# The S5 input products of a hybrid decoder trunk: plain float32, two parts per visit, in place of split products part by part

## The reference

```python
bu = jnp.einsum('blgh,gph->blgp', ug.astype(jnp.complex64), b_bar)
state = linear_scan(jnp.broadcast_to(lam_bar, bu.shape), bu)
y = jnp.einsum('blgp,ghp->blgh', state, c_c).real + d.astype(f32) * ug
```

## Time and profile before

| | |
|---|---|
| median of 3 runs | 2974.36 us (2973.3 to 2975.58) |
| profiled execution | 2973.05 us |
| its span, first to last instruction | 2971.0 us |
| mean granted TensorE clock | 0.993 |
| TensorE busy | 2894.8 us, 97% |
| VectorE busy | 2010.5 us, 68% |
| ScalarE busy | 1582.0 us, 53% |
| GpSimd busy | 751.4 us, 25% |
| DMA | 522.69 MB, mean 176 GB/s |

### The profile page before, as it was taken

The page is one execution under the profiler, slowest core; times in us unless marked ns, Lnnn a source line. Parts: engine busy times, 40 slices in busy tenths (PEclk is TensorE's granted clock), DMA queues, the critical chain, the costliest instruction groups (busy, mean ns, idle before and its releaser), DMA issues.

```text
span 2971.0 us, 56245 instructions
## 1 busy us (share of the span) xinstructions
PE 2894.8 (97%) x16280; PEld 2454.7 (83%) x16280; DVE 2010.5 (68%) x3316; ACT 1582.0 (53%) x2828; POOL 751.4 (25%) x813
## 2 busy tenths in 40 slices
PE   6999999999999999999989999999999999999997
PEld 5878888888888888888877788888888888888886
DVE  7788888755555667555568888887555555665555
ACT  5555554565555655444455554546555655644443
POOL 3145445401000123111123544543000011221110
PEclk9999999999999999999999999999999999999998
DMA  6655555655555556777745555555555555577775
GB/s 225 213 174 159 162 159 154 170 170 168 159 158 164 165 156 195 209 214 209 206 142 174 167 162 159 159 162 171 171 157 164 160 168 154 158 213 209 215 209 176
DMA packets 276414, 522.69 MB, mean 176 GB/s; under 512 B 30912, under 2 KB 33872, under 8 KB 275280
## 3 DMA queue, kind: packets, MB, share of 16 engines
q1 hardware_dynamic: 257360, 477.13, 54.8%
q10 hardware_dynamic: 18944, 44.18, 4.5%
HBM read 508.60 MB, written 16.78 MB: 177 GB/s over the span
## 4 chain that ended last, share of the span: by engine, by line
PE 46%; DVE 2%; issue 2%; ACT 1%; DVEq 0%; POOL 0%; ACTq 0%; POOLq 0%
PE ps L294 26%; PE ps L293 13%; PE ps L443 1%; PE ps L337 1%; DVE w L975 1%; PE ps L456 0%; PE ps L452 0%; PE ps L296 0%; PE ps L325 0%; PE ps L338 0%; DVE zb L1523 0%; PE ps L326 0%; PE ps L327 0%; PE ps L304 0%; PE ps L313 0%
## 5 line engine op out<-in xcount | busy, mean ns | idle before, releaser
L294 PE MATMUL ps<-hb,w 128*128 128x512 f32 x5824 | 2059.1, 396 | 7.3 <-POOL hb L1553 6.1
L975 DVE TENSOR_TENSOR w<-raw,w 128x512 fp32r<-128x512 f32 x1760 | 1290.2, 738 | 859.5 <-ACT w L590 845.1
L590 ACT ACTIVATE w<-raw 128x512 fp32r<-128x512 f32 x1760 | 1098.2, 629 | 1138.6 <-PE ps L294 1135.9
L293 PE MATMUL ps<-hb,w 128*128 128x256 f32 x5690 | 1632.4, 287 | 13.2 <-DVE w L975 11.8
L294 PEld LDWEIGHTS ps<-hb,w 128*128 128x128 f32 x5824 | 1092.9, 188 | 250.5 <-issue 6.7
L293 PEld LDWEIGHTS ps<-hb,w 128*128 128x128 f32 x5690 | 1076.0, 189 | 70.8 <-issue 29.3
L294 PE MATMUL ps<-gl,w 128*128 128x512 f32 x640 | 226.6, 395 | 0.0
L1576 POOL TENSOR_TENSOR xx<-g,tab 128x512 f32<-128x512 f32 x64 | 121.0, 1891 | 269.6 <-DVE g L1038 269.1
L1703 POOL TENSOR_TENSOR nf<-zb 128x256 f32 (+1 forms) x60 | 51.9, 864 | 537.1 <-DVE zb L1491 531.6
L294 PE MATMUL ps<-w,hb 128*128 128x512 f32 x512 | 180.8, 395 | 0.0
L293 PE MATMUL ps<-gl,w 128*128 128x256 f32 x560 | 156.6, 280 | 0.0
(11 more groups left out here) (296 smaller groups left out, 2582.1 us busy)
## 6 DMA issues: line engine op xcount, KB each, us to landing
raw<-in_w SPq DMA_DIRECT2D x1763, 256.0 KB, 2.8
mlaw<-in_mlaw ACTq DMA_DIRECT2D x16, 768.0 KB, 4.2
mlaw<-in_mlaw ACTq DMA_DIRECT2D x16, 512.0 KB, 3.5
gate<-xres ACTq DMA_DIRECT2D x32, 256.0 KB, 4.5
xres<-zb ACTq DMA_DIRECT2D x32, 256.0 KB, 3.7
zb<-in_x SPq DMA_DIRECT2D x8, 512.0 KB, 7.5
xres<-in_x SPq DMA_DIRECT2D x4, 1024.0 KB, 7.0
s5w<-in_s5w ACTq DMA_DIRECT2D x16, 256.0 KB, 3.5
```

The source lines that it names most:

```text
L293: mm(acc[:, T:], a_lo, m_hi, start=False, stop=False, skip_group_check=True)
L294: last = mm(acc, a_hi, m_both, start=(k == 0), stop=(k == nk - 1), skip_group_check=True)
L590: A(w2[:, d, :, 0, :], raw[:, s, :, :], ACT.Copy).then_inc(hi_ready, 1)
L975: V.tensor_tensor(w2[:, d, :, 1, :], raw[:, s, :, :], w2[:, d, :, 0, :].bitcast(F), ALU.subtract).then_inc(w2_ready, 1)
```

## The change

The three products on float32r halves are replaced by one plain float32 product, straight from `s5w` and from a float32 copy `us` of the inputs, still on 32 rows. A visit makes two parts: an even one into bank 4, and the odd one behind it into bank 7. There are two visits per iteration, after chunk 13 (parts 2 and 3) and after chunk 29 (parts 0 and 1 of the next iteration). `s5_split`, `bhi`, `blo` and the semaphore `us_split` are gone, and so is ScalarE's copy of the matrices; its copy of the inputs stays. `s5_next` moves from chunk 12 to chunk 17, and waits for the second visit, since the visits now read `s5w` themselves. `bu_ready` counts two per iteration in place of four.

```diff
-        us = sb("us", [P, 2, T], R)
-        bhi = sb("bhi", [P, 2, P], R)
-        blo = sb("blo", [P, 2, P], R)
+        us = sb("us", [P, T])
...
         B_BU, B_Y, B_A, B_B = 4, 5, 6, 7
+        BANKS_BU = (B_BU, B_B)
...
-            def s5_in(it, j):
-
-                if j == 0:
-                    pe.wait_ge(us_split, it * 2 + 2)
-                pe.wait_ge(bu_read, it * 4 + (j + 1))
-                r = slice(32 * j, 32 * j + 32)
+            def s5_in(it, q):
+
+                if q == 0:
+                    pe.wait_ge(s5w_loaded, it * 16 + 16)
+                    pe.wait_ge(us_ready, it + 1)
+                pe.wait_ge(bu_read, it * 4 + (2 * q + 1))
                 for a in range(2):
-                    o = ps[:, B_BU, T * a:T * a + T]
-                    mm(o, bhi[r, a, :], us[r, 0, :], start=True, stop=False)
-                    mm(o, bhi[r, a, :], us[r, 1, :], start=False, stop=False)
-                    last = mm(o, blo[r, a, :], us[r, 0, :], start=False, stop=True)
+                    for j in (2 * q, 2 * q + 1):
+                        r = slice(32 * j, 32 * j + 32)
+                        last = mm(ps[:, BANKS_BU[j % 2], T * a:T * a + T], s5w[r, a, :], us[r, :],
+                                  start=True, stop=True)
                 last.then_inc(bu_ready, 1)
...
-                steps = {5: lambda: s5_in(it, 1), 9: lambda: s5_out(it, 0), 13: lambda: s5_in(it, 2),
-                         17: lambda: s5_out(it, 1), 21: lambda: s5_in(it, 3), 25: lambda: s5_out(it, 2)}
+                steps = {9: lambda: s5_out(it, 0), 13: lambda: s5_in(it, 1),
+                         17: lambda: s5_out(it, 1), 25: lambda: s5_out(it, 2)}
...
-                act.wait_ge(bu_ready, it * 4 + 1)
-                A(us[:, 0, :], zb[:, g + Z_S5, :], ACT.Copy).then_inc(us_ready, 1)
-                act.wait_ge(s5w_loaded, it * 16 + 16)
-                A(bhi[:, :, :], s5w[:, 0:2, :], ACT.Copy).then_inc(us_ready, 1)
+                act.wait_ge(bu_ready, it * 2 + 1)
+                A(us[:, :], zb[:, g + Z_S5, :], ACT.Copy).then_inc(us_ready, 1)
...
-                act.wait_ge(us_split, it * 2 + 2)
+                act.wait_ge(bu_ready, it * 2 + 3)
                 act.wait_ge(cprime_ready, it + 1)
                 act.dma_start(s5w[:, :, :], s5w_d[it + 1]).then_inc(s5w_loaded, 16)
...
-                steps = {7: [lambda: s5_tables(it, 1)], 12: [lambda: s5_next(it)], 15: [lambda: s5_tables(it, 2)],
+                steps = {7: [lambda: s5_tables(it, 1)], 17: [lambda: s5_next(it)], 15: [lambda: s5_tables(it, 2)],
...
-                dve.wait_ge(bu_ready, it * 4 + (j + 2))
+                dve.wait_ge(bu_ready, it * 2 + (j // 2 + 2))
...
-            def s5_split(it, g):
-
-                dve.wait_ge(us_ready, it * 2 + 2)
-                V.tensor_tensor(us[:, 1, :], zb[:, g + Z_S5, :], us[:, 0, :].bitcast(F),
-                                ALU.subtract).then_inc(us_split, 1)
-                V.tensor_tensor(blo[:, :, :], s5w[:, 0:2, :], bhi[:, :, :].bitcast(F),
-                                ALU.subtract).then_inc(us_split, 1)
...
```

More of the change, by code:

```diff
@@ L191, in trunk @@
             sem("silu_ready"), sem("glu_ready"), sem("glu_tanh"), sem("glu_squared"), sem("y2_ready"))
-        us_split, s5w_loaded, s5_done = sem("us_split"), sem("s5w_loaded"), sem("s5_done")
+        s5w_loaded, s5_done = sem("s5w_loaded"), sem("s5_done")
         s5_turned, s5_sin, lam_ready, lam_exp = sem("s5_turned"), sem("s5_sin"), sem("lam_ready"), sem("lam_exp")
@@ L1016, in y_mul @@
                                 ALU.mult).then_inc(hf_ready, 1)
-            bu = ps[:, B_BU, :].rearrange("p (a t) -> p a t", a=2)
+            bu = [ps[:, b, :].rearrange("p (a t) -> p a t", a=2) for b in BANKS_BU]
             def s5_rotate(it, j):
-                dve.wait_ge(bu_ready, it * 4 + (j + 2))
+                dve.wait_ge(bu_ready, it * 2 + (j // 2 + 2))
                 dve.wait_ge(tab_ready, it * 4 + (j + 2))
                 dve.wait_ge(state_ready, it * 4 + (j + 1))
-                own.do(V.tensor_tensor(yy[:, :, :], bu, tab[:, 0:1, :].to_broadcast([P, 2, T]), ALU.mult))
+                own.do(V.tensor_tensor(yy[:, :, :], bu[j % 2], tab[:, 0:1, :].to_broadcast([P, 2, T]), ALU.mult))
             def s5_rotate2(it, j):
-                V.tensor_tensor(g2[:, :, :], bu[:, ::-1, :], tab[:, 2:0:-1, :], ALU.mult).then_inc(bu_read, 1)
+                V.tensor_tensor(g2[:, :, :], bu[j % 2][:, ::-1, :], tab[:, 2:0:-1, :], ALU.mult).then_inc(bu_read, 1)
             def s5_sum(it, j):
@@ L1078, in s5_steps @@
                 steps[3] = ([] if first else [lambda: s5_tail(it - 1, g - 1)]) + [lambda: s5_scalars(g)] + steps[3]
-                if more:
-                    steps[27] = steps[27] + [lambda: s5_split(it + 1, g + 1)]
                 return steps
@@ L1274, in _ @@
                              13: [lambda: square_up(5, 1, 5)], 14: [lambda: square_up(5, 1, 5)], 16: [s5_turns],
-                             18: [s5_scale], 20: [s5_scale2], 22: [lru_softplus],
-                             27: [lambda: s5_split(l * G8, 0)]})
+                             18: [s5_scale], 20: [s5_scale2], 22: [lru_softplus]})
                 own.restart()
```

## The result

The changed kernel takes 2941.8 us (median of 4 runs) beside 2975.0 us for the kernel before on the same chip: a ratio of 0.989 with a 95% interval of 0.9872 to 0.9907, 33 us less.

A forecast was written before the change was run, and what follows sets the result against it. TensorE, busy 97%, was taken to bound the kernel; overlapped visits give -23.2 us and VectorE's lateness +3.7, so -19.5 from 2974.4: 2955 us, 0.66% less. Range 2944 to 2975 us.

The forecast's parts named there:

- What bounds the kernel: TensorE, busy 97% of the span, alone bounds a steady S5 iteration; VectorE partly bounds a layer's first one.
- The visit of before: One `s5_in` visit on TensorE costs 1.10 us, 0.70 products and 0.40 shape changes; 64 visits take 70.4 us.
- the float32 instruction: On TensorE a float32 matmul of 256 columns is two instructions of 0.215 us each, also on few rows.
- the change of shape: Changing TensorE's matmul shape costs about 0.20 us on entering and on leaving a visit, 0.40 per visit.
- five steps: New visit's eight TensorE instructions overlap at three part changes: 1.475 us, 47.2 in all, 23.2 less; chance 0.47.
- The lower bound: Second part of a visit wholly beside the first: 1.26 us, 40.3 in all, 30.1 less; chance 0.04.
- the loss of 1.4 us in each first iteration and 0.45 in each last: VectorE's late state chain takes back part of the visits' saving in each layer's first and last iterations, together 3.7 us.
- the relief: VectorE, spared `s5_split`, gives back 0.84 us and some 0.3 of its waits in a layer's first iteration.
- No overlap (1): TensorE runs a visit's eight instructions as one stream: 2971 us, no measurable change; chance 0.26.
- Changes of rows that cost like changes of shape (2): Each of 96 row changes in TensorE's visits costs 0.20 us, +19.7 in all: 2991.5 us, slower; chance 0.13.
- VectorE taking it back (3): Overlap as forecast, but part 0 of 14 iterations waits 0.5 us for VectorE's state chain: 7 us lost, 2962 us; chance 0.10.
- The moved load and its wait: Loading the next `s5w` at ScalarE's step 17 instead of 12, waiting for the visit at chunk 13, costs 0.

The follow-up runs named there:

- The swapped loops: Changed kernel with a visit's two loops swapped, both products of the even part before both of the odd: 2942.4 us, ratio 0.9897 to the kernel before.
- the kernel with the same rows: Changed kernel, but the odd part of a visit reads the even part's rows again: 2967.7 us, ratio 0.9983 to the kernel before.
- the added subtractions: Changed kernel with two 128x256 subtractions put back on VectorE after chunk 27, into an unread spare buffer: 2946.8 us, ratio 0.991 to the kernel before.

## Why the prediction was wrong

**What bounds the kernel** held: the gain is TensorE's time, a steady iteration is TensorE's alone before and after, and VectorE matters in the first iteration of a layer only.

**The visit of before** (1.10 us), **the float32 instruction** (0.215 us) and **the change of shape** (0.40 us per visit, paid 32 times less) held: with one part alone the visit is 1.25 us for 1.26 reckoned, with eight instructions in a row 2.10 for 2.12, with float32r pairs 1.08 for 1.10.

**The step that failed is "if starts keep their order, only the first instruction of the next part can lie beside the second one of the part before".** It made five steps of a visit that has four. The swapped loops show that the order of the program doesn't hold an instruction back behind one on other rows: the instructions begin two by two in either order. That is 32 x 0.215 = 6.9 us of the error. The lower bound that I had worked out, 40.3 us for all visits, is what they cost (32 x 1.25 = 40.0), and I gave it a chance of 0.04. The Trainium skill's page "TensorE: Matmul & The Clock Gate" (Packing small matmuls — row/col tiling) has different row groups run concurrently, and the trace agrees. Its other sentence there, that matmuls start and end in program order, doesn't fit these float32 products (1.26 us per visit with the loops swapped, where that order gives 1.9), unless the two instructions of each are put in another order before they reach the array, which the records don't show.

**The second step that failed is the loss of 1.4 us in each first iteration and 0.45 in each last.** The last iterations lost nothing: from `s5_out(0)` to `s5_out(3)` they went from 39.26 to 38.34 us, where 2 x 1.10 - 1.25 = 0.95 are saved in visits. For the first ones I compare two without a long GpSimd instruction, layer 1 before and layer 0 after: 48.96 and 47.08 us, 1.88 less, all of the 4 x 1.10 - 2 x 1.25 = 1.90. The forecast was right that visits saved there don't all arrive. Between `s5_out(1)` and `s5_out(2)` one visit is gone and the stretch stays at 10.97 us. Behind `s5_out(3)`, where another is gone, 0.70 arrives. What it had too small is the relief: between `s5_out(2)` and `s5_out(3)`, with one visit in both kernels, 12.50 us become 11.16. Here TensorE had waited for the split itself, which the 2.3 us of the first line of the earlier trace rows say. In the kernel before, layers 0 and 1:

```profile
177.16 0.37 PE L325 MATMUL ps<-us,bhi 32*128 32x256 f32 x1 [0.72 <-DVE blo L1056]
...
1640.28 0.37 PE L325 MATMUL ps<-us,bhi 32*128 32x256 f32 x1 [1.60 <-DVE blo L1056]
```

The forecast counted VectorE's busy time, 0.84 us, and 0.3 of its waits. That the two sides meet at 1.9 looks like chance. In layer 1 of the changed kernel 1.3 us are lost, by GpSimd's long instruction, which the forecast didn't have. So of the 3.7 us that it took off, the traces show about 1.3; 2.4 are error.

The visits give 70.4 - 40.0 = 30.4 us, and 1.3 of it is lost; the span fell by 31.6. It is made up so: ten steady iterations of 1.95 are 19.5, the two seventh ones 4.1, the two last 1.8, the two first 2.8, and 3.4 lie before the first `s5_out`, between the layers and behind. The visits explain 1.9 of these 3.4; for the other 1.5, and for one more within the iterations, I have no account. The medians fell by 33.2, as the profiled execution of the kernel before was 1.9 us under its median, that of the changed kernel 0.3.

**The rivals.** No overlap (1) is what the kernel with the same rows measures, 2967.7 us, near the 2971 given. Changes of rows that cost like changes of shape (2) are refuted: a paired visit has several and costs what an unpaired one does, and on one and the same set of rows 2.10 us follow from the instructions alone. VectorE taking it back (3) is refuted for the steady iterations by the 0.81 us of slack and by the 52.09 us that the added subtractions leave as they are. Two figures of the rivals are off without changing them: the products of (1) come to 32 x 8 x 0.215 = 55 us, not 59, and the changes of rows of (2) to 96 x 0.20 = 19.2 us, not 19.7. The moved load and its wait cost nothing that the steady iteration shows.

## What to carry to other kernels

Where products contract over few rows, put those of different rows, behind one another in one visit: here, with two banks, two parts cost what one does, and that was worth 25 us (same rows against different rows), while plain float32 without pairing lost 7. Price a visit of small products by the distance between the large ones on its two sides, and count each change of shape. Where an engine bounds only one stage, look in the rows for the waits that name the very instruction that the change removes (here 2.3 us for `blo`) before pricing its relief at busy time. And compare such a stage more than once: here it came out 1.27 us apart in the two layers of one kernel.

## What the runs showed that I had not expected

- A float32 product of two instructions and its neighbour on other rows overlap fully, whichever of the two orders the program gives them (two by two, 0.22 us apart, in both).
- Going straight from 128 rows by 32 columns to 32 rows by 128 columns saves 0.065 us against going through the full array between them, where each change of shape costs about 0.20.
- GpSimd's and VectorE's halves of the rotation back, 128x512 each, stretch one another: 1.65 and 1.77 us, or 2.87 to 3.44 and 0.68. A long one of GpSimd made the first iteration of a layer 1.27 us longer in the changed kernel, through ScalarE's tables for the most part, and nothing longer in a steady one.
